# Retention in a two-block transformer kernel: both key slabs and the first value slab turned from eight block products to seven, with their weight sums on GpSimd and the token sums made twice

## The reference, cut to what matters

```python
def retention_mixer(h, pos, w_in, w_out):
    proj = h @ w_in                                  # 256 x 1024 @ 1024 x 6144
    q, k, v, g = jnp.split(proj, [RET_QK, 2 * RET_QK, 2 * RET_QK + RET_V], axis=-1)
    q = rotary(q.reshape(bsz, L, RET_HEADS, RET_DK), pos)
    k = rotary(k.reshape(bsz, L, RET_HEADS, RET_DK), pos) * (RET_DK ** -0.5)
    v = v.reshape(bsz, L, RET_HEADS, RET_DV)
    o = retention_chunkwise(q, k, v)
    ...
    return (jax.nn.silu(g) * o) @ w_out
```

## Time and profile before

| | |
|---|---|
| median of 3 runs | 2036.76 us (2036.74 to 2038.46) |
| the profiled execution | 2037.42 us, its span 2035.6 us |
| granted TensorE clock, mean | 0.988 of full speed |
| TensorE busy | 1927.5 us, 95% of the span |
| VectorE, ScalarE, GpSimd busy | 774.2, 394.5, 409.8 us |
| the projection of the retention | about 1200.7 to 1358.1 us of the span |

### The profile page before, as it was taken

The page is one execution under the profiler, slowest core; times in us unless marked ns, Lnnn a source line. Parts: engine busy times, 40 slices in busy tenths (PEclk is TensorE's granted clock), DMA queues, the critical chain, the costliest instruction groups (busy, mean ns, idle before and its releaser), DMA issues. The chain is left out here.

```text
span 2035.6 us, 27661 instructions
## 1 busy us (share of the span) xinstructions
PE 1927.5 (95%) x11116; PEld 1260.8 (62%) x11116; DVE 774.2 (38%) x1661; ACT 394.5 (19%) x771; POOL 409.8 (20%) x354
## 2 busy tenths in 40 slices
PE   7999999999898899988999999999999999999998
PEld 5644644443343333333443357998898888989998
DVE  3767432223122221212222145863534315452563
ACT  3125221111111111111111030221103206320221
POOL 0000000000000000000000001401794951337764
PEclk9999999999999999999999999999999999899999
DMA  9987699999999999999999995963624343334432
GB/s 374 378 297 263 234 392 406 425 423 427 428 429 428 429 429 428 428 429 429 429 429 428 423 393 199 330 233 133 210 69 155 124 173 107 125 130 172 165 120 78
DMA packets 120094, 615.60 MB, mean 302 GB/s; under 512 B 5344, under 2 KB 9568, under 8 KB 90560
## 3 DMA queue, kind: packets, MB, share of 16 engines
q1 hardware_dynamic: 118240, 604.43, 74.3%
q0 software_dynamic: 1760, 9.83, 1.3%
HBM read 613.20 MB, written 1.05 MB: 302 GB/s over the span
## 5 line engine op out<-in xcount | busy, mean ns | idle before, releaser
L1657 PE MATMUL psum<-ring,arena 128*64 128x512 f32 (+1 forms) x3200 | 687.6, 603 | 64.1 <-DMA ring<-in_w_in_dram 62.3
L1657 PEld LDWEIGHTS psum<-ring,arena 128*64 128x64 f32 (+1 forms) x3200 | 222.9, 135 | 502.4 <-issue 433.0
L1234 PE MATMUL psum<-arena,ring 128*128 128x256 f32 (+1 forms) x1440 | 326.9, 389 | 1.6 <-ACT arena L2127 0.9
L1234 PEld LDWEIGHTS psum<-arena,ring 128*128 128x128 f32 x1440 | 272.3, 190 | 53.9 <-issue 16.6
L2260 ACT ACTIVATE arena<-psum 128x512 f32<-128x512 f32 (+1 forms) x144 | 79.0, 571 | 729.4 <-PE psum L1657 725.4
L3736 POOL DMA_DIRECT2D arena<-in_pos_dram x1 | 0.5, 543 | 907.9 <-PE psum L1786 907.9
L1253 PE MATMUL psum<-arena,ring 128*128 128x128 f32 x1358 | 160.3, 276 | 1.1 <-DVE rstd L3205 0.6
L1253 PEld LDWEIGHTS psum<-arena,ring 128*128 128x128 f32 x1358 | 155.6, 192 | 3.3 <-issue 1.8
L2942 DVE TENSOR_SCALAR arena<-consts,arena 128x64 f32<-128x64 f32 (+2 forms) x64 | 15.7, 310 | 318.7 <-PE psum L1657 318.7
L3718 POOL TENSOR_TENSOR ring<-ring 128x1024 f32<-128x1024 f32 (+1 forms) x46 | 121.8, 2648 | 26.4 <-PE psum L1253 20.5
L2967 DVE TENSOR_TENSOR arena<-psum,arena 128x512 f32<-128x512 f32 x60 | 38.6, 684 | 223.4 <-PE psum L1678 223.4
(11 more groups left out here) (464 smaller groups left out, 2261.1 us busy)
## 6 DMA issues: line engine op xcount, KB each, us to landing
ring<-in_w_in_dram SPq DMA_DIRECT2D x120, 2048.0 KB, 17.1
ring<-in_w_out_dram SPq DMA_DIRECT2D x60, 2048.0 KB, 17.2
ring<-in_w_ada_dram SPq DMA_DIRECT2D x36, 2048.0 KB, 13.6
ring<-in_w_up_dram SPq DMA_DIRECT2D x22, 2048.0 KB, 8.1
ring<-in_w_ret_dram SPq DMA_DIRECT2D x12, 2048.0 KB, 19.1
ring<-in_w_down_dram SPq DMA_DIRECT2D x16, 1408.0 KB, 6.1
ring<-in_w_qkv_dram SPq DMA_DIRECT2D x4, 2048.0 KB, 20.1
ring<-in_w_in_dram SPq DMA_DIRECT2D x8, 1024.0 KB, 17.4
```

What stands on the lines that cost most here:

```text
L1234: ins = nc.tensor.matmul(bank(c)[:, at:at + n], w[:, k, m * P:m * P + P], r, start=(k == 0), stop=(k == k_tiles - 1))
L1657: ins = nc.tensor.matmul(psum[at:at + size, p, :], act[:, k, n:n + size], w, start=(k < 3 - halves), stop=(k >= KD - 3 + halves))
```

## The change

K0, K1 and V0 go by seven. Five things follow.

1. The token sums are made a first time early (`early_tokens`, in the part of `rv` that the values of slabs 2 and 3 fill later), behind the second query head, and serve K0, K1, V0, V1. They are made a second time in `gate_tokens`, where they stood before, inside V0's adds, and serve V2 and on: `rot`, which holds two of them, is needed by the turns until then.
2. GpSimd makes the weight sums of K0, K1, V0 too, ahead of those of V1 to V3, under the same rules (S4 behind product 6; S3 behind product 3 of the slab before the last, whose room it takes).
3. A key head is put together by the adds in PSUM bank 6 or 7 (`key_out`) and turned from there; one of the turn's two products goes to PSUM bank 5 (`turned_key`), so its difference and sum read `rot` once and PSUM once.
4. `state_factors` moves from behind the fourth query head to behind the third. The two whole sums of rows become four halves, in K0, K1 and (two) V0.
5. ScalarE copies product 1 of K0, K1, V0, and centers V0's value as it does the others'.

```diff
@@ TensorE @@
+            pe.wait_ge(ret_tokens, 4)
             for s in range(2):
-                features(("rk", s), lambda k: h2[:, k, :], 2)
-            arrived(("rv", 0))
-            tokens(("rv", 0), lambda k, t: h2[:, k, t * P:t * P + P], TT, BANK)
-            pe.wait_ge(ret_tokens, 4)
-            for s in range(1, 4):
+                arrived(("rk", s))
+                seven_products(("rk", s), key_weights(s), gate_blocks(early_tokens))
+            for s in range(4):
                 arrived(("rv", s))
-                seven_by_tokens(("rv", s), value_weights(s), gate_blocks())
+                if s == 2:
+                    pe.wait_ge(ret_tokens, 8)
+                seven_by_tokens(("rv", s), value_weights(s), gate_blocks(early_tokens if s < 2 else gate_tokens))
...
@@ ScalarE @@
+            for s in range(2):
+                copy_first(("rk", s), 2)
             for s in range(4):
-                if s:
-                    copy_first(("rv", s), 2)
+                copy_first(("rv", s), 2)
...
@@ VectorE @@
+            def sums_of_tokens(tokens, done):
+
+                b = gate_blocks(tokens)
+                for n, (out, x0, x1) in enumerate((("T1", "B12", "B11"), ("T3", "B22", "B12"), ("T2", "B22", "T1"),
+                                                   ("T4", "B21", "T2"))):
+                    if n > 1:
+                        dve.wait_ge(ret_tokens, done + (n if n == 3 else 1))
+                    V.tensor_tensor(b[out], b[x0], b[x1], ALU.subtract).then_inc(ret_tokens, 1)
...
+                if h == 0:
+                    state_angles()
+                if h == 1:
+                    modulation(6)
+                    copied(dve, ("cols", 6))
+                    sums_of_tokens(early_tokens, 0)
+                if h == 2:
+                    state_factors()
+
+            def turn_key(h, done):
+
+                a, b, src = two(rot[:, 0, :]), two(turned_key), key_out(h % 2)
+                own.mark(V.tensor_tensor(a, src, over_tiles(cos2, 2), ALU.mult))
+                own.link(V.tensor_tensor(b, src, over_tiles(sin2, 2), ALU.mult))
+                own.mark(V.tensor_tensor(rk[:, 2 * h, :], a[:, 0, :], b[:, 1, :], ALU.subtract))
+                V.tensor_tensor(rk[:, 2 * h + 1, :], a[:, 1, :], b[:, 0, :], ALU.add).then_inc(ret_qk, 1)
...
+            for s in range(2):
+                key = ("rk", s)
+                with_sixth_product(key, 2)
+                read_done(with_seventh_and_fifth(key, 2, key_out(1)[:, :, P:T]), (key, 5))
+                sum_of_rows(8, 4 * s, 4 * s + 4)
+                read_done(plus_product(key, 2, 2, first_product, key_out(0)[:, :, 0:P]), (key, 2))
+                read_done(plus_product(key, 4, 2, with_seventh, key_out(1)[:, :, 0:P]), (key, 4))
...
+                turn_key(2 * s + 1, RET_HEADS + 2 * s + 1)
+                read_done(plus_product(key, 3, 2, with_fifth, key_out(0)[:, :, P:T]), (key, 3))
...
+                turn_key(2 * s, RET_HEADS + 2 * s + 2)
 
             first_product, with_sixth, with_seventh, with_fifth = partial_sums["rv"]
+            key = ("rv", 0)
+            with_sixth_product(key, 2)
+            sums_of_tokens(gate_tokens, 4)
+            read_done(with_seventh_and_fifth(key, 2, value_out(0, 1, 1)), (key, 5))
+            sum_of_rows(9, 0, 4)
+            read_done(plus_product(key, 2, 2, first_product, value_out(0, 0, 0)), (key, 2))
+            read_done(plus_product(key, 4, 2, with_seventh, value_out(0, 1, 0)), (key, 4))
+            sum_of_rows(9, 4, KD)
+            read_done(plus_product(key, 3, 2, with_fifth, value_out(0, 0, 1)), (key, 3))
...
@@ GpSimd @@
             pool.wait_ge(ret_tokens, 4)
-            for s in range(1, 4):
+            for s in range(2):
+                in_place(("rk", s))
+                weight_sums(("rk", s), key_weights(s), (("rk", s), 6))
+            for s in range(4):
                 in_place(("rv", s))
-                if s == 3:
-                    read_ready(pool, (("rv", 1), 3))
+                read_ready(pool, (("rk", s) if s < 2 else ("rv", s - 2), 3))
                 weight_sums(("rv", s), value_weights(s), (("rv", s), 6))
```

More of the change, by code:

```diff
@@ L317, in plan @@
     for s in range(2):
-        slab(("rk", s), 2)
+        seven([("rk", s)])
     sums = iter(SUMMED[SUMMED_1:])
     for s, n_sums in enumerate((1, 1, 2, 2)):
-        if s:
-            seven([("rv", s)])
-        else:
-            slab(("rv", 0), 2)
+        seven([("rv", s)])
         for _ in range(n_sums):
@@ L646, in transformer_blocks_kernel @@
         partial_sums = {kind: [a[:, T * n:T * n + T] for n in range(4)]
[L647 removed]
+                        for kind, a in (("rk", flat(rstd)), ("rv", flat(rstd)), ("rg", flat(rstd)), (("up", 0), flat(rstd)), (("up", 1), spare),
                                         (("down", 1), spare))}
@@ L657, in partial @@
         def partial(key):
-            return partial_sums[key[0] if key[0] in ("rv", "rg") else key[:2]]
+            return partial_sums[key[0] if key[0] in ("rk", "rv", "rg") else key[:2]]
         def with_sums(w, sums):
@@ L667, in value_weights, with key_weights, key_out @@
         def value_weights(s):
-            return with_sums(slab(("rv", s)), value_sums[s])
+            return with_sums(slab(("rv", s)), row_sums[s % 2])
+        def key_weights(s):
+            return with_sums(slab(("rk", s)), row_sums[s])
+        def key_out(i):
+            return two(psum[:, 6 + i, :])
         def value_out(s, i, l):
@@ L678, in gate_weights, with gate_blocks @@
             return with_sums(slab(("rg", s)), gate_sums[s])
-        def gate_blocks():
+        def gate_blocks(tokens=gate_tokens):
             b = {f"B{j + 1}{l + 1}": h2[:, 4 * j:4 * j + 4, P * l:P * l + P] for j in range(2) for l in range(2)}
-            return b | {f"T{n + 1}": gate_tokens[n] for n in range(4)}
+            return b | {f"T{n + 1}": tokens[n] for n in range(4)}
         def gate_out(s, i, l):
@@ new lines, in _ @@
+            for h in range(RET_HEADS):
+                key = (("rq", h // 2), h % 2)
+                read_ready(dve, key)
+                a, b = two(rot[:, 0, :]), two(rot[:, 1, :])
+                own.mark(V.tensor_tensor(a, two(bank(key)), over_tiles(cos2, 2), ALU.mult))
+                read_done(V.tensor_tensor(b, two(bank(key)), over_tiles(sin2, 2), ALU.mult), key)
+                dve.wait_ge(dve_step, own.n)
+                copied(dve, key)
+                own.mark(V.tensor_tensor(rq[:, 2 * h, :], a[:, 0, :], b[:, 1, :], ALU.subtract))
+                V.tensor_tensor(rq[:, 2 * h + 1, :], a[:, 1, :], b[:, 0, :], ALU.add).then_inc(ret_qk, 1)
+                dve.wait_ge(dve_step, own.n)
+                dve.wait_ge(ret_qk, h + 1)
+                if h == 0:
[6 more added lines that the diff above has]
+                    state_factors()
@@ new lines, in turn_key @@
+            def turn_key(h, done):
[4 more added lines that the diff above has]
+                V.tensor_tensor(rk[:, 2 * h + 1, :], a[:, 1, :], b[:, 0, :], ALU.add).then_inc(ret_qk, 1)
+                dve.wait_ge(dve_step, own.n)
+                dve.wait_ge(ret_qk, done)
```

53 lines of the change are left out of this document (13 added, 40 removed).

## The result

On one chip the kernel before took 2037.16 us (median of 6, 2036.74 to 2038.87) and the changed kernel 2046.07 us (median of 6, 2042.76 to 2049.38), ratio 1.0035, 95% interval [1.0025, 1.0045] (the medians alone stand at 1.0044). The forecast was 2043.4 us, its range 2034.3 to 2049.0, and slower the likeliest outcome. The direction and the mechanism held; the time came out 2.7 us above the forecast, about half of it because one term was too small.

A forecast was written before the change was run, and what follows sets the result against it. TensorE, busy throughout the touched stretch, was taken as the bound. Losses of 1.7 + 4.6 + 2.05 + 1.95 + 0.6 = 10.9 us less 4.3 saved add 6.6 to 2037.4; less 0.66 for the median, 2043.4 us, range 2034.3 to 2049.0.

The forecast's parts named there:

- Saved, 4.3: K0, K1 and V0 on TensorE: by seven instead of the plain form, they save 4.3 us together.
- Backlog without a conflict: VectorE's lateness carried on without port conflict: V2 waits 1.6 us, G0 0.4, G1 0.2; 2.2 us in all.
- Who stands for whom: A VectorE instruction with two SBUF inputs waits out a whole GpSimd weight sum, up to 2.2 us; PSUM inputs aren't held.
- I take it that they alternate: Where VectorE and GpSimd run side by side: after each wait the other engine goes next; V0's token sums end 14.5 us in.
- V0, 4.6: V0: second token sums wait for weight sums, the add of 7 ends at 14.9, product 3 waits 4.6 us.
- V1 and V2, 2.05 and 1.95: V1 and V2: VectorE is still late, so product 3 waits for the add of 7, 2.05 and 1.95 us.
- K0, 1.7: K0: 0.5 us for the fourth query's late bank plus 1.2 for caught state factors, 1.7 in sum, ends 0.4 and 7.5.
- The heavier rival: K0: two or three state factors each wait out a weight sum; 4 to 6 us above forecast, 2048 to 2049; chance 0.17.
- G0 and G1, 0.6: First two gate slabs: the remaining backlog costs 0.4 us in G0 and 0.2 in G1.
- VectorE keeping the port: After waiting out one sum VectorE keeps the port for consecutive instructions; about 4.5 us lost, 2037.0 us; chance 0.14.
- no conflict: VectorE and GpSimd don't conflict on these shapes, the backlog alone costs; not slower, 2034.7 us; chance 0.14.
- the full gain: V1's 12.0 us VectorE chain is loosened somewhere and nothing waits; 4.3 us saved, 2032.4 us; chance 0.07.

The follow-up runs named there:

- the T tokens from PSUM: Changed kernel with the four second T tokens (token sums) reading their first input from PSUM, sums wrong: stage 158.30 us, whole time 2041.5 us.
- the shorter filler: Changed kernel with 11 unread products put ahead of V0's product 3 on TensorE: stage 165.79 us, whole time 2042.9 us.
- the three edits: Changed kernel with state factors behind the last gate product, token sums copied by ScalarE, ScalarE's next product 1 copied earlier: stage 152.99 us, whole time 2040.19 us.
- 16 columns: Changed kernel with the four second token sums working on 16 of 512 columns, sums wrong: stage 159.51 us, whole time 2041.3 us.
- the factors in G3: The three edits, but with state factors in gate slab G3: 2031.54 us, ratio 0.9968 to the kernel before; stage 153.60 us.

## Why the prediction was right, and where a term was short

**Saved, 4.3.** Right: K1 12.51 where a plain slab takes 13.84, and with everything in place the stage is 4.5 us shorter (0.2 of that from G1's wait).

**Backlog without a conflict.** Right to a tenth: 1.6 in V2 and 0.4 in G0 forecast, 1.56 and 0.41 with the T tokens from PSUM.

**Who stands for whom.** Right in kind: a VectorE instruction with two SBUF inputs stands out a weight sum, and one with an input from PSUM doesn't. "I take it that they alternate" was right for instructions as long as these and is not the rule, as the small ones show. It was inferred from two rows, and both had instructions long enough for GpSimd to be in line.

**V0, 4.6.** Product 3 started 4.96 us late. The add of 7 was done at 14.9 by my count; the record has it start at 14.86 and free the bank at 15.3.

**V1 and V2, 2.05 and 1.95.** In the profile of the changed kernel they look wrong, 0.49 and 1.75, and V0 looks 1.84 worse than its wait. Together the three slabs lost 9.04 us (45.31 less 3 x 12.09) where 8.6 was forecast, and with the clock held up the two terms were 2.04 and 1.92. The fall of the clock was not foreseen and did not change the sum. The prediction put each loss on product 3 alone; the profile with the shorter filler spreads V1's, 0.72 us ahead of product 6, 0.25 over 6 and 7, and 0.97 over the next three. The total is the same because the add of 7 still sets when product 3 can start.

**K0, 1.7.** This is the step that failed: "for the caught ones I take half of one, 1.2". One factor is caught in every profile of the changed kernel, 3.06 us in all. What led up to it was right to 0.1 us: less the 1.57 us by which this profile starts its stage later, the factors began at 1227.9 and S4 at 1233.5, where the prediction had 1227.8 and 1233.45. The error was to turn a coincidence that I couldn't resolve (0.2 us) into an average. By the prediction's own working an execution shows 0.5 or about 3, never 1.7. The heavier rival, with two or three caught, didn't come; its 0.17 was for a case whose first step is what happened.

**G0 and G1, 0.6.** 0.42 and about 0.1.

In sum 12.6 against 10.9, so 1.7 of the 2.7 us that the forecast was short, 1.4 of them K0's; the rest of the difference to the median, 1.0 us, lies outside the stage and within what varies there.

**The rivals.** VectorE keeping the port, no conflict, and the full gain are out by V0's rows. The last would have needed what the three edits do: they give the whole gain, and V1's 12.0 us of VectorE work in 12.09 is then still met, since nothing enters V0 late.

## What to carry to other kernels

When work moves to GpSimd, list every VectorE instruction with two SBUF inputs that will run beside it, and count a GpSimd instruction's whole length for each that is long enough for GpSimd to be in line again when it ends. A small one pays as much when it is caught, but not each is: two of four with 16 columns, one of the state factors. The cure is one input in PSUM, another engine (here ScalarE's idle 17 us), or a place where GpSimd rests. When a price hangs on whether two instructions meet, state both outcomes and choose, don't average. Follow a moved block to its new place too: the factors were worth 3 us where they left and cost 5.6 us where they first went, just outside the stretch that I was watching.

## What the runs showed of the hardware

In the stretches compared here TensorE's granted clock fell to the 1.2 GHz level at two idle times of TensorE, 4.8 us (V0) and 3.9 us (the first retention step). When it fell differs between executions of the same kernel. In the first profile of the changed kernel it stood at 0.50 from about 1272.3 us, 2.5 us into V0's wait, to 1279.1. In the second, with a wait of the same length, it fell only behind the wait's end and stood at 0.50 from 1272.5 to 1276.0, which is why V0 is 18.89 in one and 18.35 in the other. Behind the waits of 2.1 us in K0 it didn't fall.

It also falls, or doesn't, at one place that no edit touches. The changed kernel, window, length, busy, clock, DMA share, GB/s, in the first profile:

```profile
1745.00:1760.00 15.00, 14.33 (x64) 0.56 0.79 281
```

And in the second, of the same kernel:

```profile
1745.00:1760.00 15.00, 14.93 (x110) 1.00 0.75 275
```

Between matched products on either side of it, the second gained 5.8 us (16.76 against 22.51), about the distance of the two groups of runs (5.3 us). Ten of the fourteen profiles have this fall; the four without it are the second and third of the changed kernel, the one with 11 filler products and the one with the factors in G3. From the end of the stage to the end of the span these four take 673.2 us each. The others take 677 to 680, before 677.5, if the two that wait at the first retention step are left out. TensorE's last idle time ahead of the place is 0.64 to 0.67 us in all fourteen.

So 4.1 us of the lead of the kernel with the factors in G3 over the profiled execution of before (8.6 us) are this fall, not the edits. Its median may owe something to the same. Four of its eight runs took 2028.8 to 2030.2 us at a mean clock of 0.990 to 0.992, the other four 2032.9 to 2036.7 at 0.986 to 0.989, which fits a fall in some and not in others, but only one of the eight was profiled. What decides it stays open.
